# A reordered start and a tail taken by token block in an encoder block with product-key experts

## The chip, the cores and the metric

The kernel runs on one core of one Trainium2 chip. The metric is the device time of one execution in microseconds (us); lower is better. The core's engines run at the same time and are ordered by semaphores alone: PE (TensorE: matmuls, transposes), DVE (VectorE), ACT (ScalarE), POOL (GpSimd) and SP, which here only issues transfers. ACT and POOL issue transfers too.

## The reference

512 tokens of width 1024, float32. What it computes:

```python
h = layer_norm(x, ln_emb_g, ln_emb_b)
z = h @ w_in                          # 28 chunks of 128 columns
# gated short convolution: cb * conv3(cc * cx); 8 recurrent heads: two directions of
# conv4, two gates, h_t = a_t*h_{t-1} + sqrt(1-a_t^2)*i_t*x_t, with
# log a_t = -8 * r_t * softplus(-lambda)
mix = concat(rms_norm(gelu(gate) * lru), rms_norm(y_conv))
h = layer_norm(ALPHA * h + mix @ w_out, ln1_g, ln1_b)
# experts: per token and each of 8 query heads the best 16 of 128*128 experts by key sums
y = sum over the 128 chosen e of gate_e * gelu(h . u_e) * v_e
out = layer_norm(ALPHA * h + y, ln2_g, ln2_b)
```

## The kernel before, in words

Activations are split into four token blocks of 128. Products of float32 operands are made as three passes, hi*hi, hi*lo and lo*hi: ACT writes the rounded half of a tile ("hi"), another engine subtracts it to get the rest ("lo").

**Start and mixer** (`mixer`, lines 163 to 647). DVE takes moments of each token block (`stats`) and normalises it, POOL makes the inverse roots, PE turns the block (L135). ACT scales each of the eight 128x512 turned tiles (`shape`, L144), DVE splits each into hi (L150) and lo (L152). The first product `z_chunk(0)` takes each tile as it comes. The weights of chunk n come by SP into one of three buffers; ACT rounds them (`w_upper`, L339), and POOL subtracts (`w_lower`, L267). Chunks alternate between two PSUM banks, so chunk n waits until chunk n-2's bank has been read. Order of the chunks: four groups j of three (0 to 11) for the short convolution, then two for each head. In a group j, ACT copies the first chunk (L379), DVE multiplies it with the second (L477), convolves (L483, L485) and multiplies with the third (L487). Every engine works in program order. Ahead of group 0, DVE's program has the 21 small dependent operations for softplus of lambda (L456 to L467, 128x16 each), which only the heads use. POOL, beside `w_lower`, applies gain and shift to one token block in two operations (L295, L297) in chunks 2 to 9. The parameter vectors are turned by PE in one transpose each (L564, L565), put ahead of the last token block's transposes; ACT copies them out (L347, L348) after `w_upper(1)`, and the scaling needs them. The gain and shift rows of the first norm (`ln`) and the gate weights are issued on ACT's queue before its first rounding.

**Experts** (`experts`, from L1295). Token blocks 0 to 2 (`DT` = 3) are taken densely over all 128 blocks of 128 experts: 128 steps, each for one V block. A step makes w = activations * gates (DVE, L1571), rounds it (ACT, L1500) and the V block (ACT, L1481), subtracts (DVE, L1576 and L1549), and PE adds 18 matmuls of 128x512 (L1451) into six PSUM banks, two for each token block. V blocks have four slots (`SLOT`), so V block n+4 is rounded when step n's matmuls are done; v_hi and v_lo of n+2 are made in step n, ahead of the w halves of step n. Token block 3 goes by gathered rows: one gather in DVE's program at each step up to step 111; the next 16 steps have none.

**The end.** After the steps, DVE adds the gathered sums to block 3 (L1586, L1588), and then for each block in turn: two operations that add PSUM (L1596), moments (L1600, L1602); POOL makes scale and shift in four small operations (L1536 to L1539); ACT normalises (L1509); gain and shift are applied by DVE on 768 columns and by POOL on 256 (`affine`, L1378, L1379); SP stores. `y_ready` rises for a token block when its matmuls of the last step are done.

Of the kernel before, what the change touches and what calls it, by code (L numbers as in the profile page):

```python
# [22 lines left out]
F32 = mybir.dt.float32  # L23
# [8 lines left out]
P = 128  # L32
# [123 lines left out]
def mixer(nc, a, sem, bank, h, ident, ones, iota, small, pB):  # L156
    V, S, G = nc.vector, nc.scalar, nc.gpsimd
    with ExitStack() as st:
# [71 lines left out]
        with nc.Block() as block:  # L230
            @block.sync
            def _(eng):
                for tb in range(TB):
                    eng.dma_start(h[:, tb, :], a["x"][0, tb * P:(tb + 1) * P, :]).then_inc(x_loaded[tb], 16)
                for n, c in enumerate(order):
                    after(eng, w_lo_ready, n - NW + 1)
                    eng.dma_start(wbuf[n % NW][:, :, :],
                                  a["w_in"][0, :, c * P:(c + 1) * P].rearrange("(k p) c -> p k c", p=P)
                                  ).then_inc(w_loaded[n % NW], 16)
                    for c in rows_with(n):  # L240
                        eng.dma_start(wo[:, c, :], a["w_out"][0, c * P:(c + 1) * P, :]).then_inc(wo_loaded, 16)

            @block.gpsimd
            def _(eng):
# [68 lines left out]
            def _(eng):  # L313
# [13 lines left out]
                for i, name in enumerate(("ln_emb_g", "ln_emb_b")):  # L327
                    eng.dma_start(ln[:, i, :], a[name].partition_broadcast(P)).then_inc(ln_loaded, 16)
# [90 lines left out]
            def _(eng):  # L419
# [35 lines left out]
                eng.wait_ge(exp_lam, 2)  # L455
                link(V.tensor_scalar(out=s, in0=e, scalar1=2.0, scalar2=None, op0=ALU.add))  # L456
                link(V.reciprocal(s, s))
                link(V.tensor_tensor(out=s, in0=s, in1=e, op=ALU.mult))
                link(V.tensor_tensor(out=s2, in0=s, in1=s, op=ALU.mult))
                link(V.tensor_scalar(out=poly, in0=s2, scalar1=1.0 / 15, scalar2=1.0 / 13, op0=ALU.mult, op1=ALU.add))  # L460
                for k in (11, 9, 7, 5, 3, 1):
                    link(V.tensor_tensor(out=poly, in0=poly, in1=s2, op=ALU.mult))
                    link(V.tensor_scalar(out=poly, in0=poly, scalar1=1.0 / k, scalar2=None, op0=ALU.add))
                link(V.tensor_tensor(out=poly, in0=poly, in1=s, op=ALU.mult))
                link(V.tensor_scalar(out=neg, in0=neg, scalar1=0.0, scalar2=LRU_C / 2, op0=ALU.max, op1=ALU.mult))
                link(V.scalar_tensor_tensor(out=sp[:, 0, :], in0=poly, scalar=LRU_C, in1=neg, op0=ALU.mult, op1=ALU.add))
                V.tensor_scalar(out=sp[:, 1, :], in0=sp[:, 0, :], scalar1=-1.0, scalar2=None,  # L467
                                op0=ALU.mult).then_inc(sp_ready, 1)


                eng.wait_ge(xp_zero, 1)
                for j in range(CONV):
# [16 lines left out]
                    V.sem_inc(y_ready, 1)  # L489

# [801 lines left out]
def experts(nc, a, sem, bank, h, small, acts, far, act_dram, gates_dram, out):  # L1292
# [9 lines left out]
    STEPS = KEYS  # L1302
    GATHERS = 2 * TURN
# [4 lines left out]
    assert u_turns * GATHERS == SLOTS - U_FROM and 0 <= tail_tiles <= STEPS - TAIL  # L1308
    LAST = (DT, *range(DT))
    LEFT, RIGHT = slice(0, 6 * P), slice(6 * P, D)  # L1310
# [10 lines left out]
    with ExitStack() as st:  # L1321
# [13 lines left out]
        shift = sb("shift2", [P, TB, 1])  # L1335
# [7 lines left out]
        ln2_loaded, var_ready, rstd_ready, norm_ready, stored = (sem(n) for n in (  # L1343
            "ln2_loaded", "var2_ready", "rstd2_ready", "norm2_ready", "out_stored"))
        y_ready, left_ready, right_ready = sem("y_block_ready"), sem("out_left_ready"), sem("out_right_ready")
        chain, pool_chain = sem("dve_chain_experts"), sem("pool_chain_experts")
# [38 lines left out]
        with nc.Block() as block:  # L1385
            @block.sync
            def _(eng):
# [50 lines left out]
            def _(eng):  # L1438
                mm = nc.tensor.matmul

                def outputs(n, i):

                    first, last = (isinstance(n, int) and n == e for e in (0, STEPS - 1))
                    r = i % SLOT
                    eng.wait_ge(v_lo_ready, n + 1)
                    eng.wait_ge(w_lo_ready, n + 1)
                    for tb in range(DT):
                        for w, v, begins, ends in ((w_hi, v_hi, first, False), (w_hi, v_lo, False, False),
                                                   (w_lo, v_hi, False, last)):
                            for half in range(2):  # L1450
                                ins = mm(bank[2 + 2 * tb + half][:, :], w[r][:, tb * P:(tb + 1) * P],  # L1451
# [176 lines left out]
```

## Time and profile before

| | us |
|---|---|
| median of 3 runs | 1784.73 (1784.1 to 1785.97) |
| profiled execution, its own time | 1783.23 |
| its span, first to last instruction | 1781.4 |
| PE busy | 1683.2 (94%) |
| DVE busy | 1327.9 (75%) |
| ACT busy | 664.6 (37%) |
| POOL busy | 741.0 (42%) |
| mean granted TensorE clock | 0.973 of full speed |

Busy shares are means over stages with different limits. Where PE has no idle time, PE sets the pace, and nothing on another engine shortens the stage; where it is idle, the row tells what it waited for. Times on the rows below are us from the span's start.

### The profile page before, as it was taken

To read this page: it belongs to the slowest core of one execution; us is meant where nothing else is said; L and a number is where in the kernel's file an instruction comes from. 1 tells how busy PE (TensorE), PEld (TensorE's weight loads), DVE (VectorE), ACT (ScalarE), POOL (GpSimd) and SP (SyncE) were. 2 spreads that over 40 slices of the span, in tenths; PEclk is the share of its full clock that TensorE was granted. 3 is DMA by queue.
4 is the path that set the end of the run, shared out by engine and by line. 5 is a ranking of instruction groups with operands and counts; after the bars stand their busy time and mean duration, and the time that the engine had idled before them with its cause. 6 is when DMAs were issued, how large, how long until landed. Compare 5 with 4: busy or idle time off the path is not lost. (4 is left out here: it accounts for less than half of the span.)

```text
span 1781.4 us, 26976 instructions
## 1 busy us (share of the span) xinstructions
PE 1683.2 (94%) x8781; PEld 1462.4 (82%) x8781; DVE 1327.9 (75%) x2584; ACT 664.6 (37%) x1034; POOL 741.0 (42%) x690
## 2 busy tenths in 40 slices
PE   5999989799998999999999988999999999999995
PEld 4786644489998999899999987888888888888884
DVE  7469962458888888688779817778777778888756
ACT  3457760243334334233323323333333333333332
POOL 5635430194432211221145404444666667555303
PEclk8999999899999999999999998999999999999997
DMA  7422100333323666965988899999999989999971
GB/s 262 128 79 71 54 0 0 121 97 113 113 78 103 196 190 201 372 190 178 312 300 256 273 325 348 326 318 319 320 323 319 319 294 331 363 356 356 320 229 57
DMA packets 224427, 396.75 MB, mean 223 GB/s; under 512 B 15256, under 2 KB 155472, under 8 KB 224336
## 3 DMA queue, kind: packets, MB, share of 16 engines
q1 hardware_dynamic: 182512, 258.12, 43.2%
q0 software_dynamic: 36864, 134.23, 22.1%
q10 hardware_dynamic: 4960, 3.24, 0.6%
q8 instruction: 50, 0.82, 0.2%
q14 instruction: 41, 0.34, 0.1%
HBM read 349.40 MB, written 46.14 MB: 222 GB/s over the span
## 5 line engine op out<-in xcount | busy, mean ns | idle before, releaser
L709 PE MATMUL bank<-xhi,ut_hi 128*128 128x384 f32 x1024 | 355.6, 347 | 0.0
L709 PE MATMUL bank<-xhi,ut_lo 128*128 128x384 f32 x1024 | 344.4, 336 | 0.0
L709 PE MATMUL bank<-xlo,ut_hi 128*128 128x384 f32 x1024 | 344.4, 336 | 0.0
L801 POOL COPY row_index<-expert_rows 128x1 int32<-128x1 int32 (+1 forms) x256 | 158.3, 618 | 425.4 <-DVE gather_product L819 343.8
L1451 PE MATMUL bank<-v_hi,w_hi 128*128 128x512 f32 x768 | 241.0, 395 | 3.8 <-DVE w_lo L1576 3.8
L1451 PE MATMUL bank<-v_lo,w_hi 128*128 128x512 f32 x768 | 238.0, 391 | 0.0
L1451 PE MATMUL bank<-v_hi,w_lo 128*128 128x512 f32 x768 | 237.5, 391 | 0.0
L1481 ACT ACTIVATE v_hi<-v_raw 128x1024 fp32r<-128x1024 f32 x128 | 135.6, 1060 | 244.0 <-PE bank L1451 236.3
L767 DVE TENSOR_TENSOR ut_lo<-bank,ut_hi 128x512 fp32r<-128x512 f32 x216 | 141.5, 684 | 113.6 <-ACT ut_hi L726 112.4
L806 POOL DMA_INDIRECT gathered<-in_peer_v,row_index x128 | 179.4, 1401 | 106.2 <-POOLq L805 102.8
L1549 DVE TENSOR_TENSOR v_lo<-v_raw,v_hi 128x1024 fp32r<-128x1024 f32 x128 | 156.3, 1221 | 70.8 <-ACT v_hi L1481 70.8
L709 PEld LDWEIGHTS bank<-xlo,ut_hi 128*128 128x128 f32 x1024 | 194.1, 190 | 0.0
L709 PEld LDWEIGHTS bank<-xhi,ut_hi 128*128 128x128 f32 x1024 | 194.1, 190 | 0.0
L709 PEld LDWEIGHTS bank<-xhi,ut_lo 128*128 128x128 f32 x1024 | 193.4, 189 | 0.0
L806 POOL DMA_INDIRECT gathered<-in_peer_u,row_index x128 | 143.5, 1121 | 107.0 <-POOLq L805 101.9
L726 ACT ACTIVATE ut_hi<-bank 128x512 fp32r<-128x512 f32 x256 | 144.9, 602 | 78.2 <-PE bank L697 77.9
L697 PE MATMUL bank<-ident,u_raw 128*128 128x128 f32 x1024 | 142.6, 278 | 29.2 <-DVE ut_lo L767 14.7
L1451 PEld LDWEIGHTS bank<-v_lo,w_hi 128*128 128x128 f32 x768 | 144.8, 189 | 30.9
L1451 PEld LDWEIGHTS bank<-v_hi,w_lo 128*128 128x128 f32 x768 | 144.7, 188 | 30.9
L1451 PEld LDWEIGHTS bank<-v_hi,w_hi 128*128 128x128 f32 x768 | 142.6, 189 | 32.0 <-DVE v_lo L1549 4.2
L819 DVE SCALAR_TENSOR_TENSOR gather_product<-gathered,h 128x1024 f32<-128x1024 f32 x128 | 156.2, 1220 | 9.8 <-DMA gathered<-in_peer_u,row_index 4.7
L823 DVE SCALAR_TENSOR_TENSOR gather_sum<-gathered,expert_gates,gather_sum 128x1024 f32<-128x1024 f32 x128 | 160.5, 1278 | 2.5 <-DMA gathered<-in_peer_v,row_index 2.5
(182 smaller groups left out, 2697.7 us busy)
## 6 DMA issues: line engine op xcount, KB each, us to landing
u_raw<-in_peer_u SPq DMA_DIRECT2D x128, 512.0 KB, 4.8
v_raw<-in_peer_v SPq DMA_DIRECT2D x128, 512.0 KB, 6.0
g_in<-gate_matrix SPq DMA_DIRECT2D x128, 192.0 KB, 4.2
activations<-gel SPq DMA_DIRECT2D x96, 192.0 KB, 2.9
a_in<-activations SPq DMA_DIRECT2D x96, 192.0 KB, 4.5
gate_matrix<-stage SPq DMA_DIRECT2D x15, 1152.0 KB, 8.2
w_in<-in_w_in SPq DMA_DIRECT2D x28, 512.0 KB, 3.8
wq<-in_peer_wq SPq DMA_DIRECT2D x16, 512.0 KB, 4.2
```

The costliest lines, as they stand in the source:

```text
L697: ins = self.nc.tensor.transpose(self.bank[b][:, k * P:(k + 1) * P], raw[:, j * P:(j + 1) * P], self.ident[:, :])
L709: ins = self.nc.tensor.matmul(self.bank[b + (r % 2) * spare][:, 0:DTOK], u[r % 2][:, k, :], x[:, k, 0:DTOK], start=(i == 0), stop=(i == 3 ...
L726: ins = self.nc.scalar.activation(self.hi[r % 2][at], turned, ACT.Copy)
L767: self.nc.vector.tensor_tensor(out=self.lo[r % 2][at], in0=self.bank[b].rearrange("p (k e) -> p k e", k=4), in1=self.hi[r % 2][at].bitcast ...
L801: nc.gpsimd.tensor_copy(self.index[r][:, :], self.rows[:, bass.ds(k, 1)]).then_inc(self.index_ready, 1)
L806: nc.gpsimd.indirect_dma_start(out=self.tile[r][:, :], out_offset=None, in_=self.tables[kind], in_offset=bass.IndirectOffsetOnAxis(ap=self ...
L819: ins = V.scalar_tensor_tensor(out=self.product[:, :], in0=self.tile[r][:, :], scalar=1.0, in1=self.x, op0=ALU.mult, op1=ALU.mult, accum_o ...
L823: ins = V.scalar_tensor_tensor(out=y, in0=self.tile[r][:, :], scalar=self.gate[:, bass.ds(k, 1)], in1=y, op0=ALU.mult, op1=ALU.add)
L1451: ins = mm(bank[2 + 2 * tb + half][:, :], w[r][:, tb * P:(tb + 1) * P], v[r][:, half * HALF_D:(half + 1) * HALF_D], start=begins, stop=ends)
L1481: S.activation(v_hi[r][:, :], v_raw[r][:, :], ACT.Copy).then_inc(v_hi_ready, 1)
L1549: V.tensor_tensor(out=v_lo[r][:, :], in0=v_raw[r][:, :], in1=v_hi[r][:, :].bitcast(F32), op=ALU.subtract).then_inc(v_lo_ready, 1)
```

## The change

At the start: `w_lower(0)` and `w_lower(1)` go from POOL to DVE, the first ahead of the eight splits and the second between the fourth and the fifth. `w_upper(1)` goes behind the second scaled tile. The turns of the parameters go ahead of token block 2 in place of 3. The two `ln` transfers go to SP's queue behind the third weight transfer; the gate weights stay on ACT's queue, behind the eight scalings. The softplus goes from before group 0 to behind group 2.

At the end: the last four steps (`CLOSE` = 124) are multiplied by token block, all four V blocks for block 0, then 1, then 2, so that block 0's sums are final 48 matmuls before the last. For that, V block 127 is rounded and subtracted in step 126 behind w, not in 125. Token block 3 is finished in six parts in steps 112 to 117. The norm is on DVE, with POOL for the power alone: (h - mean) * gain in one operation, * root + shift in two halves, each stored as it comes; ACT has no part in it.

```diff
@@ -237,6 +237,9 @@
                     eng.dma_start(wbuf[n % NW][:, :, :],
                                   a["w_in"][0, :, c * P:(c + 1) * P].rearrange("(k p) c -> p k c", p=P)
                                   ).then_inc(w_loaded[n % NW], 16)
+                    if n == NW - 1:
+                        for i, name in enumerate(("ln_emb_g", "ln_emb_b")):
+                            eng.dma_start(ln[:, i, :], a[name].partition_broadcast(P)).then_inc(ln_loaded, 16)
...
@@ -282,11 +285,10 @@
                 for tb in range(TB):
                     invert_root(tb)
                 G.memset(xp[:, :, :], 0.0).then_inc(xp_zero, 1)
-                w_lower(0)
-                w_lower(1)
                 eng.wait_ge(ln_ready, 1)
                 eng.wait_ge(turner.turned, KD)
+                eng.wait_ge(w_lo_ready, 2)
...
-                for i, name in enumerate(("ln_emb_g", "ln_emb_b")):
-                    eng.dma_start(ln[:, i, :], a[name].partition_broadcast(P)).then_inc(ln_loaded, 16)
...
-                load_gate_weights(0)
-                load_gate_weights(1)
                 link = Chain(eng, act_chain)
                 w_upper(0)
-                w_upper(1)
                 eng.wait_ge(pT_ready, 1)
                 S.activation(pB[:, :], bank[7][:, last][:, 0:PC_END], ACT.Copy)
                 S.activation(pA[:, :], bank[6][:, last], ACT.Copy).then_inc(p_ready, 1)
                 eng.wait_ge(p_ready, 1)
                 for k in range(KD):
+                    if k == 2:
+                        w_upper(1)
                     turner.shape(eng, k)
+                load_gate_weights(0)
+                load_gate_weights(1)
...
+                def w_lower(n):
+                    eng.wait_ge(w_hi_ready, n + 1)
+                    V.tensor_tensor(out=w_lo[n % 2][:, :, :], in0=wbuf[n % NW][:, :, :],
+                                    in1=w_hi[n % 2][:, :, :].bitcast(F32), op=ALU.subtract).then_inc(w_lo_ready, 1)
+                w_lower(0)
                 for k in range(KD):
+                    if k == 4:
+                        w_lower(1)
                     turner.split(eng, k)
...
-                eng.wait_ge(exp_lam, 2)
-                link(V.tensor_scalar(out=s, in0=e, scalar1=2.0, scalar2=None, op0=ALU.add))
...
+                def softplus():
+                    eng.wait_ge(exp_lam, 2)
+                    link(V.tensor_scalar(out=s, in0=e, scalar1=2.0, scalar2=None, op0=ALU.add))
+                    link(V.reciprocal(s, s))
...
+                    if j == CONV - 2:
+                        softplus()
...
-                    if tb == TB - 1:
+                    if tb == TB - 2:
...
-                        if tb == TB - 1 and k == 6:
+                        if tb == TB - 2 and k == 6:
...
+    CLOSE = STEPS - SLOT
+    FAR_DONE = TAIL + tail_tiles
...
-        def affine(eng, engine, link, at, cols, ready):
-            blk = h[:, LAST[at], cols]
-            eng.wait_ge(norm_ready, at + 1)
-            link(engine.tensor_tensor(out=blk, in0=blk, in1=ln[:, 0, cols], op=ALU.mult))
-            engine.tensor_tensor(out=blk, in0=blk, in1=ln[:, 1, cols], op=ALU.add).then_inc(ready, 1)
...
-                    for cols, ready in ((RIGHT, right_ready), (LEFT, left_ready)):
-                        eng.wait_ge(ready, at + 1)
+                    for half in range(2):
+                        cols = slice(half * HALF_D, (half + 1) * HALF_D)
+                        eng.wait_ge(out_ready, 2 * at + half + 1)
                         eng.dma_start(out[0, tb * P:(tb + 1) * P, cols], h[:, tb, cols]).then_inc(stored, 16)
...
+                def block_outputs(tb, r, first, last):
+                    for w, v, begins, ends in ((w_hi, v_hi, first, False), (w_hi, v_lo, False, False),
+                                               (w_lo, v_hi, False, last)):
+                        for half in range(2):
+                            ins = mm(bank[2 + 2 * tb + half][:, :], w[r][:, tb * P:(tb + 1) * P],
+                                     v[r][:, half * HALF_D:(half + 1) * HALF_D], start=begins, stop=ends)
+                    return ins
+                def closing():
+                    for tb in range(DT):
+                        for n in range(CLOSE, STEPS):
+                            if tb == 0:
+                                eng.wait_ge(v_lo_ready, n + 1)
+                                eng.wait_ge(w_lo_ready, n + 1)
+                            ins = block_outputs(tb, n % SLOT, False, n == STEPS - 1)
+                        ins.then_inc(y_ready, 1)
...
-                outputs(STEPS - 1, STEPS - 1)
+                closing()
...
-                    if not (isinstance(n, int) and n + 2 >= STEPS):
+                    if not (isinstance(n, int) and n + 2 >= STEPS - 1):
...
+                    if isinstance(n, int) and n == STEPS - 2:
+                        v_upper(n + 1, i + 1, (n + 1) // SLOT + 1)
...
-                for at, tb in enumerate(LAST):
-                    eng.wait_ge(rstd_ready, at + 1)
-                    S.activation(h[:, tb, :], h[:, tb, :], ACT.Identity, scale=rs[:, tb, :],
-                                 bias=shift[:, tb, :]).then_inc(norm_ready, 1)
...
-                        link(G.tensor_tensor(out=rs[:, tb, :], in0=mv[:, tb, 1:2], in1=small[:, 2:3], op=ALU.add))
-                        link(G.tensor_tensor(out=rs[:, tb, :], in0=rs[:, tb, :], in1=small[:, 0:1], op=ALU.pow))
-                        link(G.tensor_tensor(out=shift[:, tb, :], in0=mv[:, tb, 0:1], in1=rs[:, tb, :], op=ALU.mult))
-                        G.tensor_tensor(out=shift[:, tb, :], in0=shift[:, tb, :], in1=small[:, 1:2],
-                                        op=ALU.mult).then_inc(rstd_ready, 1)
...
+                for at, tb in enumerate(LAST):
+                    eng.wait_ge(var_ready, at + 1)
+                    G.tensor_tensor(out=rs[:, tb, :], in0=rs[:, tb, :], in1=small[:, 0:1],
+                                    op=ALU.pow).then_inc(rstd_ready, 1)
...
-                    if not (isinstance(n, int) and n + 2 >= STEPS):
+                    if not (isinstance(n, int) and n + 2 >= STEPS - 1):
...
+                    if isinstance(n, int) and n == STEPS - 2:
+                        v_lower(n + 1, i + 1)
...
+                    if isinstance(n, int) and FAR_DONE <= n < FAR_DONE + 6:
+                        far_block(n - FAR_DONE)
+                link = Chain(eng, chain)
+                def moments(tb):
+                    for i in range(2):
+                        ins = V.bn_stats(bn[:, tb, i, :], h[:, tb, i * HALF_D:(i + 1) * HALF_D])
+                    link(ins)
+                    link(V.bn_aggr(mv[:, tb, :], bn[:, tb, :, :].rearrange("p a b -> p (a b)")))
+                    V.tensor_scalar(out=rs[:, tb, :], in0=mv[:, tb, 1:2], scalar1=LN_EPS, scalar2=None,
+                                    op0=ALU.add).then_inc(var_ready, 1)
+                def centre(tb):
+                    link(V.scalar_tensor_tensor(out=h[:, tb, :], in0=h[:, tb, :], scalar=mv[:, tb, 0:1], in1=ln[:, 0, :],
+                                                op0=ALU.subtract, op1=ALU.mult))
+                def spread(tb):
+                    eng.wait_ge(rstd_ready, LAST.index(tb) + 1)
+                    for half in range(2):
+                        cols = slice(half * HALF_D, (half + 1) * HALF_D)
+                        V.scalar_tensor_tensor(out=h[:, tb, cols], in0=h[:, tb, cols], scalar=rs[:, tb, :],
+                                               in1=ln[:, 1, cols], op0=ALU.mult, op1=ALU.add).then_inc(out_ready, 1)
+                def far_block(part):
+                    if part == 1:
+                        link(V.scalar_tensor_tensor(out=h[:, DT, :], in0=h[:, DT, :], scalar=ALPHA, in1=far.sum[0][:, :],
+                                                    op0=ALU.mult, op1=ALU.add))
+                    elif part == 2:
+                        link(V.tensor_tensor(out=h[:, DT, :], in0=h[:, DT, :], in1=far.sum[1][:, :], op=ALU.add))
+                    elif part == 3:
+                        moments(DT)
+                    elif part == 4:
+                        eng.wait_ge(ln2_loaded, 32)
+                        centre(DT)
+                    elif part == 5:
+                        spread(DT)
...
-                for at in range(TB + 1):
-                    if at < TB:
-                        tb = LAST[at]
-                        if at:
-                            eng.wait_ge(y_ready, at)
-                            for i in range(2):
-                                blk = h[:, tb, i * HALF_D:(i + 1) * HALF_D]
-                                ins = V.scalar_tensor_tensor(out=blk, in0=blk, scalar=ALPHA, in1=bank[2 + 2 * tb + i][:, :],
-                                                             op0=ALU.mult, op1=ALU.add)
-                            link(ins)
-                        for i in range(2):
-                            ins = V.bn_stats(bn[:, tb, i, :], h[:, tb, i * HALF_D:(i + 1) * HALF_D])
-                        link(ins)
-                        V.bn_aggr(mv[:, tb, :], bn[:, tb, :, :].rearrange("p a b -> p (a b)")).then_inc(var_ready, 1)
-                    if at:
-                        affine(eng, V, link, at - 1, LEFT, left_ready)
+                for tb in range(DT):
+                    eng.wait_ge(y_ready, tb + 1)
+                    for i in range(2):
+                        blk = h[:, tb, i * HALF_D:(i + 1) * HALF_D]
+                        ins = V.scalar_tensor_tensor(out=blk, in0=blk, scalar=ALPHA, in1=bank[2 + 2 * tb + i][:, :],
+                                                     op0=ALU.mult, op1=ALU.add)
+                    link(ins)
+                    moments(tb)
+                    centre(tb)
+                    spread(tb)
```

## Rows read from the trace of the kernel before

**Rows 1.** The page: an engine's busy time; a group, with mean ns.
```profile
PE 1683.2 (94%) x8781; PEld 1462.4 (82%) x8781; DVE 1327.9 (75%) x2584; ACT 664.6 (37%) x1034; POOL 741.0 (42%) x690
...
L1549 DVE TENSOR_TENSOR v_lo<-v_raw,v_hi 128x1024 fp32r<-128x1024 f32 x128 | 156.3, 1221 | 70.8 <-ACT v_hi L1481 70.8
```

**Rows 2.** Waits of PE, whole run: us in total, times, longest.
```profile
PE bank L585 <- DVEq L478: 7.9, 1, 7.9
```

**Rows 3.** Windows: length, busy time of each engine, PEclk, DMA share, GB/s.
```profile
39.50:47.50 8.00, 0.08 (x2) 0.04 (x1) 7.47 (x14) 1.06 (x1) 5.26 (x3) 0.63 0.91 314
47.50:51.50 4.00, 4.00 (x10) 3.13 (x11) 2.62 (x4) 0.00 (x0) 0.00 (x0) 0.50 0.38 146
```

**Rows 4.** Timeline, 29 to 47 us: start, length, engine, line, operation.
```profile
29.45 0.18 DVE L456 TENSOR_SCALAR t<-t 128x16 f32<-128x16 f32 x1 [0.28 <-ACT t L353]
...
30.54 2.40 POOL L267 TENSOR_TENSOR w_in_lo<-w_in,w_in_hi 128x1024 fp32r<-128x1024 f32 x1 [11.34 <-ACT w_in_hi L339]
...
30.57 2.39 DVE L462 TENSOR_TENSOR t<-t 128x16 f32<-128x16 f32 x1
...
46.48 0.17 DVE L467 TENSOR_SCALAR sp<-sp 128x16 f32<-128x16 f32 x1
```

**Rows 5.** Timeline of ACT, 34 to 56 us: roundings of weights.
```profile
34.17 1.06 ACT L339 ACTIVATE w_in_hi<-w_in 128x1024 fp32r<-128x1024 f32 x1 [3.32 <-PE bank L585]
39.61 1.06 ACT L339 ACTIVATE w_in_hi<-w_in 128x1024 fp32r<-128x1024 f32 x1 [4.38 <-PE bank L585]
55.23 1.06 ACT L339 ACTIVATE w_in_hi<-w_in 128x1024 fp32r<-128x1024 f32 x1 [14.56 <-PE bank L585]
```

**Rows 6.** Timeline of DVE around the end of group 2.
```profile
84.04 0.69 DVE L487 TENSOR_TENSOR y<-hd,bank 128x512 f32<-128x512 f32 x1
94.29 0.69 DVE L477 TENSOR_TENSOR xp<-dw,bank 128x512 f32<-128x512 f32 x1 [9.56 <-PE bank L585]
```

**Rows 7.** Timeline of POOL beside it.
```profile
83.56 2.72 POOL L267 TENSOR_TENSOR w_in_lo<-w_in,w_in_hi 128x1024 fp32r<-128x1024 f32 x1
89.91 2.41 POOL L267 TENSOR_TENSOR w_in_lo<-w_in,w_in_hi 128x1024 fp32r<-128x1024 f32 x1 [3.63 <-ACT w_in_hi L339]
```

**Rows 8.** Timeline, 12 to 28 us, of DVE.
```profile
13.26 1.42 DVE L431 TENSOR_SCALAR h<-h,mv,rs 128x1024 f32<-128x1024 f32 x1 [0.71 <-POOL rs L262]
17.90 1.58 DVE L150 CAST hT_hi<-dq 128x512 fp32r<-128x512 f32 x1 [3.21 <-ACT dq L144]
...
20.58 0.69 DVE L152 TENSOR_TENSOR hT_lo<-dq,hT_hi 128x512 fp32r<-128x512 f32 x1
...
26.95 0.69 DVE L152 TENSOR_TENSOR hT_lo<-dq,hT_hi 128x512 fp32r<-128x512 f32 x1
```

**Rows 9.** Timeline, 12 to 18 us, of PE, then of ACT.
```profile
14.74 0.87 PE L135 MATMUL bank<-ident,h 128*128 128x128 f32 x6
15.72 1.06 ACT L339 ACTIVATE w_in_hi<-w_in 128x1024 fp32r<-128x1024 f32 x1 [3.69 <-DMA w_in<-in_w_in]
```

**Rows 10.** Window over the last five steps.
```profile
1740.00:1759.70 19.70, 19.70 (x87) 15.97 (x86) 12.37 (x19) 4.65 (x7) 1.15 (x4) 1.00 0.06 18
```

**Rows 11.** Timeline of the halves of w in step 126.
```profile
1746.19 0.55 DVE L1571 TENSOR_TENSOR w<-a_in,g_in 128x384 f32<-128x384 f32 x1
...
1746.78 0.53 ACT L1500 ACTIVATE w_hi<-w 128x384 fp32r<-128x384 f32 x1 [1.81 <-DVE w L1571]
...
1747.34 0.56 DVE L1576 TENSOR_TENSOR w_lo<-w,w_hi 128x384 fp32r<-128x384 f32 x1 [0.59 <-ACT w_hi L1500]
```

**Rows 12.** Timeline of the end, 1753 to 1776 us.
```profile
1753.93 0.57 POOL L1537 TENSOR_TENSOR rs<-rs,small 128x1 f32<-128x1 f32 x1
...
1757.03 1.28 DVE L1596 SCALAR_TENSOR_TENSOR h<-h,bank 128x512 f32<-128x512 f32 x2 [3.56 <-PE bank L1451]
...
1760.83 1.28 POOL L1537 TENSOR_TENSOR rs<-rs,small 128x1 f32<-128x1 f32 x1
...
1774.74 1.32 POOL L1379 TENSOR_TENSOR h<-h,ln 128x256 f32<-128x256 f32 x1
```

More of the change, by code:

```diff
@@ L461, in _ @@
[L461 to L466, printed above, removed]
@@ L467, in _ @@
-                V.tensor_scalar(out=sp[:, 1, :], in0=sp[:, 0, :], scalar1=-1.0, scalar2=None,
-                                op0=ALU.mult).then_inc(sp_ready, 1)
+                def softplus():
+                    eng.wait_ge(exp_lam, 2)
+                    link(V.tensor_scalar(out=s, in0=e, scalar1=2.0, scalar2=None, op0=ALU.add))
+                    link(V.reciprocal(s, s))
+                    link(V.tensor_tensor(out=s, in0=s, in1=e, op=ALU.mult))
+                    link(V.tensor_tensor(out=s2, in0=s, in1=s, op=ALU.mult))
+                    link(V.tensor_scalar(out=poly, in0=s2, scalar1=1.0 / 15, scalar2=1.0 / 13, op0=ALU.mult, op1=ALU.add))
+                    for k in (11, 9, 7, 5, 3, 1):
+                        link(V.tensor_tensor(out=poly, in0=poly, in1=s2, op=ALU.mult))
+                        link(V.tensor_scalar(out=poly, in0=poly, scalar1=1.0 / k, scalar2=None, op0=ALU.add))
+                    link(V.tensor_tensor(out=poly, in0=poly, in1=s, op=ALU.mult))
+                    link(V.tensor_scalar(out=neg, in0=neg, scalar1=0.0, scalar2=LRU_C / 2, op0=ALU.max, op1=ALU.mult))
+                    link(V.scalar_tensor_tensor(out=sp[:, 0, :], in0=poly, scalar=LRU_C, in1=neg, op0=ALU.mult, op1=ALU.add))
+                    V.tensor_scalar(out=sp[:, 1, :], in0=sp[:, 0, :], scalar1=-1.0, scalar2=None,
+                                    op0=ALU.mult).then_inc(sp_ready, 1)
@@ L1307, in experts @@
     assert TURNS * SLOT == KEYS - MADE and GATHERS % RING == 0 and 2 < u_turns < TURNS - 1
-    assert u_turns * GATHERS == SLOTS - U_FROM and 0 <= tail_tiles <= STEPS - TAIL
+    FAR_DONE = TAIL + tail_tiles
+    assert u_turns * GATHERS == SLOTS - U_FROM and 0 <= tail_tiles and FAR_DONE + 6 <= CLOSE
     LAST = (DT, *range(DT))
-    LEFT, RIGHT = slice(0, 6 * P), slice(6 * P, D)
     is_live = lambda n, i: i % 2 == 0 and (not isinstance(n, int) or n < TAIL)
@@ L1334, in experts @@
         rs = sb("rs2", [P, TB, 1])
-        shift = sb("shift2", [P, TB, 1])
         v_loaded = [sem(f"v_loaded{i}") for i in range(SLOT)]
@@ L1342, in experts @@
         y_done = sem("y_step_done")
[L1343 to L1346, printed above, removed]
+        ln2_loaded, var_ready, rstd_ready, stored = (sem(n) for n in (
+            "ln2_loaded", "var2_ready", "rstd2_ready", "out_stored"))
+        y_ready, out_ready = sem("y_block_ready"), sem("out_half_ready")
+        chain = sem("dve_chain_experts")
         def steps(eng, step, between=lambda: None):
@@ L1441, in outputs @@
                 def outputs(n, i):
-                    first, last = (isinstance(n, int) and n == e for e in (0, STEPS - 1))
-                    r = i % SLOT
+                    first = isinstance(n, int) and n == 0
                     eng.wait_ge(v_lo_ready, n + 1)
@@ L1447, in outputs @@
                     for tb in range(DT):
[L1448 to L1451, printed above, removed]
-                                         v[r][:, half * HALF_D:(half + 1) * HALF_D], start=begins, stop=ends)
-                        if last:
-                            ins.then_inc(y_ready, 1)
-                    if not last:
-                        ins.then_inc(y_done, 1)
+                        ins = block_outputs(tb, i % SLOT, first, False)
+                    ins.then_inc(y_done, 1)
+                def block_outputs(tb, r, first, last):
[13 more added lines that the diff above has]
+                        ins.then_inc(y_ready, 1)
                 def step(n, i, t, tiles):
@@ L1466, in step @@
                             acts.turn_half(eng, 1, m + 1, r + 1, (r + 1) // acts.UB + 1 + t, 0, 0)
-                    if not (isinstance(n, int) and n == 0):
+                    if not (isinstance(n, int) and (n == 0 or n > CLOSE)):
                         outputs(n - 1, i - 1)
                 steps(eng, step)
-                outputs(STEPS - 1, STEPS - 1)
+                closing()
             @block.scalar
```

17 lines of the change are left out of this document (removed).

## The prediction

> **What bounds the kernel now.** I read the page's busy times first: PE is busy for 1683.2 of 1781.4 us [rows 1], so only what PE waits for, what it does slowly, and what lies behind its last matmul can be worth microseconds. The waits of PE come next. Among them one wait of 7.9 us at the head of a weight chunk stands for DVE's queue [rows 2]. The window around it shows PE with 0.08 us of work in 8.0 us while DVE is busy for 7.47, and in the 4.0 us behind it a granted clock of 0.50, that is 1.2 instead of 2.4 GHz [rows 3]. The timeline tells what DVE does there: the softplus, 21 dependent operations of 0.17 to 0.25 us that begin at 29.45 and end at 46.65 [rows 4]. Chunk 3 needs the bank that DVE's first product of group 0 reads, and this product stands behind the softplus. Last, the end: PE is done by 1759.7 [rows 10], the last result is there at 1776.06 [rows 12], the span ends at 1781.4.
>
> **The change part by part, the softplus.** Chunks 1 and 2 without a wait are 39.61 - 34.17 = 5.44 us apart by the roundings that follow them. Chunk 3 takes 55.23 - 39.61 = 15.62 us [rows 5]. With the softplus gone from its place, DVE has the product ready within a microsecond of chunk 1's end, some 4 us before chunk 3 wants the bank: 15.62 - 5.44 = **10.2 us** go, 8 of idle time and 2.2 of low clock. What is late next is `w_lower(3)` on POOL, and behind it in each chunk one of the gain or shift operations; a POOL operation of this size takes 2.4 to 2.7 us [rows 4, 7], so two of them fit a chunk of 5.44 by 0.0 to 0.6 us. I take nothing for it, as each is queued only behind the last, and keep 4 us (1 us in four chunks) as the bound below; 10.2 is the bound above.
>
> In its new place the softplus follows the last product of group 2, which ends at 84.04 + 0.69 = 84.73, and DVE is free until 94.29 [rows 6]. What it takes there: 21 steps of 0.21 are 4.4 us. It took 17.2 before, since POOL was at work nearly all that time: one small operation that begins 0.03 us behind a POOL operation of 2.40 us takes 2.39 us [rows 4]. Beside the new place POOL has two operations, 83.56 to 86.28 and 89.91 to 92.32 [rows 7], which can hold one small operation each: 4.4 + 1.6 + 2.4 = 8.4 us, under the 9.56 that are free. So nothing. Should it last longer, the product of group 3 can still be 5.4 us late, until chunk 12 wants its bank.
> The Trainium skill has this as a rule (SBUF — State Buffer, "Who interferes with whom"): DVE and GpSimd share a port pair that whoever starts first holds for the whole instruction, and the other fully blocks. The row of 2.39 beside 2.40 us agrees. By this rule the cost follows from the number of POOL operations in the window; if sharing slowed every small operation in proportion, the softplus would take its 17.2 us again and the sum would be the first rival's.
>
> **The start.** Now: normalisation of block 3 ends at 13.26 + 1.42 = 14.68; ACT rounds the second weights at 15.72, when they have landed, and scales only then, so that DVE's first split begins at 17.90 and takes 1.58 beside POOL; the later splits come every (26.95 - 20.58) / 6 = 1.06 us; the last ends at 27.64 [rows 8, 9]. After: `w_lower(0)` on DVE from 14.7; its nearest row is v_lo, the same shape and engine, 1.22 us [rows 1]: until 15.9. ACT has the parameters by then, because PE turned them two transposes earlier, and the first scaling can follow PE's turns from 14.74 on [rows 9]. Split 0 to 17.0, three more at 1.06 and about 0.3 for ACT's rounding of the second weights (1.06 us [rows 9]) between two scalings: 20.5. `w_lower(1)` to 21.7, four splits to 25.95. Gain 27.64 - 25.95 = **1.7 us**. The ends: the parameters' loads land only just before the time at which they are turned now (0.9 us later than I take), or chunk 0 runs wholly at the low clock (24 matmuls at 0.43 instead of 0.23 us, which ends 0.3 us behind the splits): 0.5. Without the 0.66 us by which block 3's normalisation is held, and with ACT's rounding hidden: 2.8. The edits that move work onto other queues cost nothing by this: SP's queue carries the `ln` rows (2 x 512 KB) ahead of the fourth weights, which it now issues only when `w_lo` 0 is done (15.9), and what uses `ln` comes after the splits. ACT issues four gate weight loads of 0.5 us behind the last scaling, 24.7 to 26.7, while its next work, the exponential, waits for DVE until about 27.4. If that cover were gone, each microsecond would come off the 1 us by which `w_lower(2)` is early for chunk 2. DVE's two subtractions are inside the sum above.
>
> **The end.** PE's 72 matmuls of the last four steps take 72 x 0.2265 us (87 in 19.70 us [rows 10]) = 16.3, so they begin at 1743.4. Block 0 wants V blocks 124, 125, 126 in 3 x 6 matmuls = 4.1 us and w and V of block 127 at 1747.5. Spacing w to w_hi to w_lo to the next w is 0.59, 0.56, 0.47 us [rows 11]. Step 125 no longer waits for V 127: w(125) at 1742.11, one step ahead of the 1746.19 of the row, then w_lo(125) 1743.26 (wanted 1744.8), w(126) 1743.73, w_hi 1744.32, V 127 rounded to 1745.9 (1.06), subtracted to 1747.1, w_lo(127) from 1748.2 to 1748.75. So PE waits **1.3 us** once; bounds 0 and 2.6 (each operation of this chain later by a semaphore). Then block 0 is final at 1750.2 and PE ends at 1761.0 instead of 1759.7.
> DVE from 1750.4: two additions of PSUM 1.32 (1.28 for the pair [rows 12]) and two moments, of the same size, 1.32; aggregate 0.24, epsilon 0.10, centre 1.23 (1024 columns, as v_lo [rows 1]), the root, two halves of output 0.60 each: the power takes 0.57 us alone, but 1.28 where DVE has operations on two SBUF tiles beside it [rows 12], so it is held until the centring ends and then takes some 0.5. Sum 5.9 us a block. That is more than PE's 24 matmuls (5.44), so DVE sets the end: 1750.4 + 3 x 5.9 = 1768.1. Before it was 1774.74 + 1.32 = 1776.06, for this stage is served serially, all four blocks and ACT and POOL in the chain. 8.0 us, and 0.4 for one transfer of 256 KB last in place of two of 128 and 384: **8.4 us**. Bounds: root hidden, so that PE sets the pace and only one block of 5.4 us follows 1761.0, 9.9; root wholly behind the centring (6.7 us a block) and the wait 2.6 us, 4.7. The six parts for block 3 lie in steps in which a gather of 1.2 to 1.3 us is missing from DVE; each part is at most 1.7 us, and the step has more idle time than the difference. If not, some tenths.
>
> **The sum** against the profiled execution: 1783.23 - 1.7 - 10.2 - 8.4 = 1762.9. The median of the runs shown is 1.5 above this execution: **1764.4 us**. All low ends give 0.5 + 6.2 + 4.7 = 11.4 (1773.3), all high ends 2.8 + 10.2 + 9.9 = 22.9 (1761.8).
>
> **Rivals.** First, the softplus doesn't fit its new place. For it: DVE's and POOL's operations interlock, and the wait of 17.2 us was made so. At 17.2 us it ends at 101.9, 2.2 us behind the 99.7 at which chunk 12 wants the bank; with the product 0.7 and a low clock of up to 2.2 us behind the gap, 3 to 5 us come back: 1767.4 to 1769.4, say 1768.4. Against it: only two POOL operations there. Second, the 11.9 us of the start are lost again later, as the stage of the heads or a stage with loads takes its pace from something that doesn't move. Then the end alone remains: 1784.7 - 8.4 = 1776.3. Against it: every load is issued after a semaphore of the work before it, so all of it moves together. Third, slower: the clock. PE got 1.2 GHz after the gap [rows 3], and with chunk 0 now paced by splits that pause for `w_lower(1)`, it might stay there. Each chunk of 24 matmuls costs 24 x 0.2 = 4.8 us more; the change is slower once this lasts over four chunks, and at six it stands at 1764.4 + 28.8 = 1793.2. Against it: chunk 3 is back at full speed before its end.
>
> **How the numbers follow.** Forecast 0.77 (its own range 1760 to 1768), first rival 0.12, second 0.07, third 0.04. The range for 8 in 10 takes forecast and first rival and the ends of the unknown costs: from the high ends' 1761.8, less the 1.9 us over which the three runs spread, to the low ends' 1773.3, so 1760 to 1773. About 0.2% (3.6 us) is what a measurement of this kernel can tell from no change. Faster by more: forecast and the first two rivals, 0.95; within it: 0.01, a mix of second rival and a dear end; slower: 0.04.
>
> **What would show it.** Chunk 3's matmuls follow chunk 2's without a gap and at 2.4 GHz; the softplus lies between two group products and takes 7 to 9 us; the last split ends near 26; one wait of about 1.3 us in the first token block of the closing; three DVE rounds of 5.9 us, the power beginning with the centring and ending behind it. The prediction is wrong if PE shows a new wait over 2 us in chunks 1 to 12, or if the DVE rounds take over 6.5 us.

## The result and the profile after

The changed kernel takes 1764.49 us in the median of 4 runs (1762.95 to 1766.34); before 1784.99 (1784.1 to 1785.97, 4 runs). The ratio is 0.9882, with a 95% interval from 0.9871 to 0.9894: 20.5 us or 1.2% less. A second set of runs gave 1765.04 and 0.9873 (0.9858 to 0.9888).

The profiled execution took 1766.34 us itself, the slowest of its four, with a span of 1764.5; that of before, at 1783.23, was faster than all four timed ones. So the two spans stand only 16.9 us apart. The part of the traces that makes this difference is told at the end of this section.

The page of after, beside [rows 1]:

```profile
PE 1676.8 (95%) x8781; PEld 1456.0 (83%) x8781; DVE 1329.9 (75%) x2594; ACT 659.4 (37%) x1030; POOL 730.2 (41%) x668
```

**The softplus.** ACT's roundings of weights in the trace of after; the three shown follow chunks 2, 3 and 12:

```profile
37.51 1.06 ACT L339 ACTIVATE w_in_hi<-w_in 128x1024 fp32r<-128x1024 f32 x1 [4.38 <-PE bank L598]
42.95 1.06 ACT L339 ACTIVATE w_in_hi<-w_in 128x1024 fp32r<-128x1024 f32 x1 [4.38 <-PE bank L598]
...
93.71 1.06 ACT L339 ACTIVATE w_in_hi<-w_in 128x1024 fp32r<-128x1024 f32 x1 [4.24 <-PE bank L598]
```

Before, the roundings that follow chunks 0 and 12:

```profile
29.32 1.05 ACT L339 ACTIVATE w_in_hi<-w_in 128x1024 fp32r<-128x1024 f32 x1
...
105.99 1.06 ACT L339 ACTIVATE w_in_hi<-w_in 128x1024 fp32r<-128x1024 f32 x1 [4.24 <-PE bank L585]
```

The step of 15.62 of [rows 5] is now 5.44, like its neighbours. The rounding at 93.71 stood at 105.99 before: the program gets through the first chunk of the heads 12.3 us earlier. Of these, 2.1 are there at chunk 0 already (27.22 against 29.32), and 10.2 come between the two marks. The window [rows 3] has no mate any more: from 28 to 110 us PE waits for nothing. DVE in the new place of the softplus, beside [rows 6] (start, length, line), with one operation of POOL:

```profile
65.92 2.41 POOL L270 TENSOR_TENSOR w_in_lo<-w_in,w_in_hi 128x1024 fp32r<-128x1024 f32 x1 [0.73 <-ACT w_in_hi L339]
...
66.05 2.56 DVE L494 TENSOR_SCALAR hd<-xp,pB 128x512 f32<-128x512 f32 x1 [0.57 <-DVE xp L488]
...
74.28 0.69 DVE L498 TENSOR_TENSOR y<-hd,bank 128x512 f32<-128x512 f32 x1
75.23 0.17 DVE L468 TENSOR_SCALAR t<-t 128x16 f32<-128x16 f32 x1 [0.26 <-DVE y L498]
...
77.82 2.27 DVE L475 TENSOR_SCALAR t<-t 128x16 f32<-128x16 f32 x1
...
81.59 0.17 DVE L479 TENSOR_SCALAR sp<-sp 128x16 f32<-128x16 f32 x1
82.01 0.69 DVE L488 TENSOR_TENSOR xp<-dw,bank 128x512 f32<-128x512 f32 x1 [0.24 <-PE bank L598]
```

The 21 operations take from 75.23 to 81.76, 6.5 instead of 17.2 us, and one of them is held, for 2.27 us. Group 2's last product ended late, 10.2 us after its first (64.79 to 74.97) instead of 7.7, as one more of its operations met POOL (2.56 us at 66.05). The same two operations before, where the group's first product began at 77.07:

```profile
77.91 0.49 DVE L483 TENSOR_SCALAR hd<-xp,pB 128x512 f32<-128x512 f32 x1 [0.16 <-DVE xp L477]
...
78.19 2.46 POOL L267 TENSOR_TENSOR w_in_lo<-w_in,w_in_hi 128x1024 fp32r<-128x1024 f32 x1 [0.74 <-ACT w_in_hi L339]
```

POOL's operation stands where it stood, 1.1 us behind the group's first product. DVE's begins 0.4 us later than before, now just behind POOL's instead of just ahead of it, and is held. This is so in all six traces with the whole new start and in none of the other five; what delays it is not shown. So the softplus ended only 0.25 us before group 3's product could begin.

**The start.** DVE and then ACT, beside [rows 8, 9]:

```profile
12.93 1.42 DVE L432 TENSOR_SCALAR h<-h,mv,rs 128x1024 f32<-128x1024 f32 x1 [0.71 <-POOL rs L265]
14.27 1.20 DVE L444 TENSOR_TENSOR w_in_lo<-w_in,w_in_hi 128x1024 fp32r<-128x1024 f32 x1
15.66 0.43 DVE L150 CAST hT_hi<-dq 128x512 fp32r<-128x512 f32 x1 [0.19 <-ACT dq L144]
...
24.86 0.69 DVE L152 TENSOR_TENSOR hT_lo<-dq,hT_hi 128x512 fp32r<-128x512 f32 x1
```

```profile
14.85 1.45 ACT L144 ACTIVATE dq<-bank,pB 128x512 f32<-128x512 f32 x2 [1.81 <-PE bank L135]
```

The scalings begin at 14.85, the weights are subtracted on DVE in 1.20 us, the first split begins at 15.66 and the last ends at 25.55; before, 27.64. Block 3's normalisation begins at 12.93 instead of 13.26; in the eleven traces it begins at 12.93 to 13.26, so this third of a microsecond is not the edit's. From it to the rounding behind chunk 0 it is 14.3 us instead of 16.1: 1.8 us are the edit's. A window over chunk 0, of after and then of before (the last three numbers are PEclk, DMA share, GB/s):

```profile
20.00:24.00 4.00, 2.58 (x9) 1.45 (x9) 3.90 (x8) 2.04 (x3) 0.00 (x0) 1.00 0.64 216
```

```profile
20.30:24.30 4.00, 3.95 (x9) 3.14 (x10) 3.86 (x8) 3.11 (x4) 0.00 (x0) 0.50 1.06 362
```

Chunk 0 ran at 2.4 GHz; before, its first 4 us were at 1.2. Ahead of its first matmul PE had been idle for 1.45 us, before for 2.8. From 17 to 21 us, the granted clock is 1.00 in all seven traces with the reordered start and 0.50 to 0.73 in the four with the old one.

**The end.** PE's only wait in the closing, POOL's power, and DVE's rounds, beside [rows 12]:

```profile
1740.68 0.69 PE L1462 MATMUL bank<-v_hi,w_hi 128*128 128x512 f32 x2 [1.34 <-DVE w_lo L1583]
```

```profile
1745.47 1.52 POOL L1548 TENSOR_TENSOR rs<-rs,small 128x1 f32<-128x1 f32 x1 [45.57 <-DVE rs L1600]
```

```profile
1739.98 0.56 DVE L1583 TENSOR_TENSOR w_lo<-w,w_hi 128x384 fp32r<-128x384 f32 x1 [0.59 <-ACT w_hi L1518]
1742.34 1.28 DVE L1638 SCALAR_TENSOR_TENSOR h<-h,bank 128x512 f32<-128x512 f32 x2 [1.81 <-PE bank L1462]
...
1745.30 1.28 DVE L1605 SCALAR_TENSOR_TENSOR h<-h,mv,ln 128x1024 f32<-128x1024 f32 x1
1747.10 1.42 DVE L1613 SCALAR_TENSOR_TENSOR h<-h,rs,ln 128x512 f32<-128x512 f32 x2 [0.52 <-POOL rs L1548]
1748.43 1.28 DVE L1638 SCALAR_TENSOR_TENSOR h<-h,bank 128x512 f32<-128x512 f32 x2
...
1759.25 1.42 DVE L1613 SCALAR_TENSOR_TENSOR h<-h,rs,ln 128x512 f32<-128x512 f32 x2 [0.52 <-POOL rs L1548]
```

The last half of w is ready at 1740.54, PE waits 1.34 us, and DVE's rounds begin at 1742.34, 1748.43 and 1754.50, 6.08 us apart. The last result is there at 1760.67, and the span ends 3.8 us later, instead of 5.3.

**Where the two traces differ besides.** The rounding of the first V block, by the tile's rows (count, durations, first and last start), of after and of before:

```profile
L1499 ACT ACTIVATE v_hi<-v_raw x128: 1046/1061/1065, 1057.6 to 1736.6; 128x1024 fp32r<-128x1024 f32 x128
```

```profile
L1481 ACT ACTIVATE v_hi<-v_raw x128: 1047/1061/1065, 1067.3 to 1743.5; 128x1024 fp32r<-128x1024 f32 x128
```

Here the lead is 9.7 us, after 12.3 at the heads. In step 124, it is 8.1 (V block 126 is rounded at 1731.28 against 1739.41), and the new end adds 8.8. The traces of the experiments tell whether the 4.2 us in between are the change's.

### The profile page after: what moved, and what is told of

Same layout as the page of the kernel before. It is cut to its first block and busy times, and to the rows that moved or that the text cites. A ratio compares the mean times of both kernels' runs of the same rounds, so it can differ in the third digit from the quotient of the medians.

```text
span 1764.5 us, 26964 instructions
## 1 busy us (share of the span) xinstructions
PE 1676.8 (95%) x8781; PEld 1456.0 (83%) x8781; DVE 1329.9 (75%) x2594; ACT 659.4 (37%) x1030; POOL 730.2 (41%) x668
## 5 line engine op out<-in xcount | busy, mean ns | idle before, releaser
L710 PE MATMUL bank<-ident,u_raw 128*128 128x128 f32 x1024 | 141.3, 276 | 30.9 <-DVE ut_lo L780 12.3
```

The source lines that it names most:

```text
L710: ins = self.nc.tensor.transpose(self.bank[b][:, k * P:(k + 1) * P], raw[:, j * P:(j + 1) * P], self.ident[:, :])
```

## The experiments

**The start alone, the end alone.**

```diff
 start_only: mixer() of after, experts() of before
 end_only:   mixer() of before, experts() of after
```

> The kernel before with the whole reordered start and the old end. Theory A (the parts add up, nothing behind the start gives time back): the two traces put the roundings that follow chunk 13 at 105.99 and 93.71 us, so 12.3 us less than before, about 1772.7. Theory B (the stages behind the start give back part of it: the same two traces stand 12.3 us apart at the heads and only 8.1 us apart at the last four steps): 8 us less, about 1777. In the trace, the gap of 7.9 us ahead of chunk 3 is gone under both.

Measured: 1774.95 us (6 runs, 1770.35 to 1777.61) against 1785.84 of before (17 runs); ratio 0.9939 (0.9926 to 0.9951), 10.9 us less. (The rounding that the expectation puts behind chunk 13 is the one behind chunk 12.)

> The kernel before with the new end alone. Theory A: the end is worth what the trace of the changed kernel shows behind the last four steps' begin, 8.8 us, about 1776.2, and the end is the same to 0.1 us: one wait of 1.3 us on PE, three rounds of 6.1 us on DVE. Theory B about the start says the same here; a rival for the end (part of its gain comes from the phase in which the shifted program meets its loads) gives 5 to 7 us.

Measured: 1776.88 us; ratio 0.9950 (0.9937 to 0.9963), 9.0 us less. The product of the two ratios is 0.9889, and the whole gave 0.9882 and 0.9873: the parts add up. Theory B's 8 us for the start are below the interval (8.8 to 13.2), and the next row shows what misled it. The first V block's rounding in the trace of the end alone, whose program is that of before up to there:

```profile
L1486 ACT ACTIVATE v_hi<-v_raw x128: 1045/1061/1065, 1070.7 to 1747.4; 128x1024 fp32r<-128x1024 f32 x128
```

The same program reaches this point at 1067.3 in one execution and at 1070.7 in another. Of the six traces with the whole new start it is reached at 1055.5 to 1060.8, mean 1058.2; the two old ones have a mean of 1069.0. The lead is 10.8 on the mean, where it was 12.7 at chunk 12 on the mean of the same traces. From chunk 12's rounding to this one, before took 961.3 us, the shortest of all eleven traces; the ten others took 961.8 to 966.9, with the softplus in its old place (963.9, 964.5 and 963.9) as well as in its new one. So the loss in the pair above is within what the stage varies by, and the traces cannot tell 1.9 us of loss from none. The same holds for the 1.6 us behind it: from this rounding to that of V block 126, before took 672.1 and after 673.7, and the eleven traces 670.7 to 673.7.

**The softplus alone, the reordered start alone.**

```diff
 softplus_only: before, and
+                def softplus():            # the 21 operations, unchanged
...
+                    if j == CONV - 2:
+                        softplus()
 reorder_only: mixer() of after, and
-                    if j == CONV - 2:
-                        softplus()
+                softplus()                 # ahead of group 0
```

> The kernel before with the 21 small operations moved behind group 2 and nothing else. Theory A: 15.62 - 5.44 = 10.2 us less, about 1774.8, chunk 3 right behind chunk 2 at 2.4 GHz. Rival (the wait ahead of chunk 3 would be taken over by POOL's subtraction, and the early start is what gives POOL its slack): 6 to 8 us less.

Measured: 1773.9 us; ratio 0.9933 (0.9921 to 0.9946), 11.9 us less. Its roundings behind chunks 2 and 3 (5.44 apart) and chunk 12:

```profile
39.37 1.06 ACT L339 ACTIVATE w_in_hi<-w_in 128x1024 fp32r<-128x1024 f32 x1 [4.38 <-PE bank L587]
44.81 1.06 ACT L339 ACTIVATE w_in_hi<-w_in 128x1024 fp32r<-128x1024 f32 x1 [4.38 <-PE bank L587]
...
95.57 1.06 ACT L339 ACTIVATE w_in_hi<-w_in 128x1024 fp32r<-128x1024 f32 x1 [4.24 <-PE bank L587]
```

105.99 - 95.57 = 10.4 us by the trace, of which 0.2 were there at chunk 0 (29.10 against 29.32), so 10.2 between the two marks. The rival's 6 to 8 us are below the interval (9.6 to 14.1). The softplus in this trace, its two held operations and group 3's product behind it:

```profile
74.57 1.32 DVE L457 TENSOR_SCALAR t<-t 128x16 f32<-128x16 f32 x1 [0.26 <-DVE y L487]
...
79.57 2.36 DVE L466 TENSOR_SCALAR t<-t 128x16 f32<-128x16 f32 x1
...
83.87 0.69 DVE L477 TENSOR_TENSOR xp<-dw,bank 128x512 f32<-128x512 f32 x1 [1.52 <-PE bank L587]
```

With only this edit made, POOL's operations at 73.15 and 79.49 hold one each, the softplus takes 7.8 us (74.57 to 82.34), and 1.5 are to spare.

> The kernel before with all of the reordered start but the softplus, which stays ahead of group 0. Theory A: all of the start moves by 2.1 us and the wait of about 8 us ahead of chunk 3 stays: 2.1 us less, about 1782.9. Rival (the softplus meets POOL's operations at another phase and ends at the same time as before): 0 to 1 us less.

Measured: 1784.73 us in 11 runs; ratio 0.9996 (0.9988 to 1.0005), 0.7 us less, from 2.1 less to 0.9 more. The wait stays; PE's waits of this run, and its transposes of the parameters:

```profile
PE bank L597 <- DVEq L490: 7.9, 1, 7.9
```

```profile
12.72 0.48 PE L576 MATMUL bank<-ident,prow 128*128 128x128 f32 x1 [0.59 <-DMA prow<-in_lru_lambda]
...
13.41 3.50 PE L135 MATMUL bank<-ident,h 128*128 128x128 f32 x16
```

This trace gained only 1.25 us (the rounding after chunk 0 at 28.07 against 29.32; in the six other traces with the new start 27.22 to 27.39). PE waited 0.59 us for the last of the twelve parameter loads, and its transposes end 1.4 us later (16.91 against 15.51). The late load alone doesn't explain it. PE waits 0.4 to 0.5 us for it in three of the six other traces too, and they lose nothing. Start_only:

```profile
12.69 0.33 PE L577 MATMUL bank<-ident,prow 128*128 128x128 f32 x1 [0.53 <-DMA prow<-in_lru_lambda]
...
13.15 1.09 PE L135 MATMUL bank<-ident,h 128*128 128x128 f32 x8
```

Its turns behind the wait take 1.09 us for eight, against 3.50 for sixteen in reorder_only, and its rounding after chunk 0 stands at 27.24. In after the turns are slow as well (2.96 for sixteen), but it has no wait. So the loss is there only where the late load and slow turns come together; why the turns are slow in some executions, at a granted clock of 1.00 in all three, is not shown. Beside 11.9 for the softplus and 10.9 for both, the timed runs cannot tell the reordering's share from zero; the traces show it up to the heads.

**POOL's other work taken away.**

```diff
 pool_quiet: before, and
-                    if n // 2 <= TB:       # L295, L297: gain and shift
...
+                    if n // 2 <= TB and n % 2 == 1:
+                        eng.sem_inc(h_ready, 1)
```

> The kernel before, with the softplus in its old place, and without POOL's gain and shift on the residual in chunks 2 to 9 (this part of the computation is left out; its time is read for the softplus alone). If each POOL operation holds at most one of DVE's small operations for its whole length, the softplus now meets one or two of the weight subtractions (2.4 us each) in place of seven operations: it takes 4.4 us and 2.4 to 4.8, so 7 to 9 us instead of 17.2, ends by 38.5 and PE's wait ahead of chunk 3 is gone. Rival (the small operations are slow for themselves, one after another at 0.8 us): 17 us, and the wait stays 7.9.

Measured: one run, 1774.38 us, the span 1772.6. DVE's softplus in its old place (first operation, the two held ones, the last), and then POOL:

```profile
29.18 0.17 DVE L452 TENSOR_SCALAR t<-t 128x16 f32<-128x16 f32 x1 [0.28 <-ACT t L349]
...
30.31 2.38 DVE L458 TENSOR_TENSOR t<-t 128x16 f32<-128x16 f32 x1
...
35.23 2.25 DVE L461 TENSOR_SCALAR t<-t 128x16 f32<-128x16 f32 x1
...
37.73 0.17 DVE L463 TENSOR_SCALAR sp<-sp 128x16 f32<-128x16 f32 x1
```

```profile
30.27 2.39 POOL L267 TENSOR_TENSOR w_in_lo<-w_in,w_in_hi 128x1024 fp32r<-128x1024 f32 x1 [11.34 <-ACT w_in_hi L335]
35.03 2.42 POOL L267 TENSOR_TENSOR w_in_lo<-w_in,w_in_hi 128x1024 fp32r<-128x1024 f32 x1 [2.38 <-ACT w_in_hi L335]
```

8.7 us instead of 17.2. The two operations that are held, 2.38 and 2.25 us, are those beside the two POOL operations, which begin at 30.27 and 35.03; all others take 0.17 to 0.25. PE's wait ahead of chunk 3 is gone. The softplus was slow by POOL alone, one operation held for each of POOL's. The count in before fits too, though the expectation has it one too high: beside the softplus stand six POOL operations (30.54 to 45.38), and six of the 21 are held, for 2.25 to 2.39 us each. Fifteen at 0.21 and six at 2.34 make the 17.2.

**The order of the closing, DVE's order in it, the root.**

```diff
 no_closing: after, and
-                closing()
+                for tb in range(DT):      # the last step; outputs(n - 1) in every step before it
+                    block_outputs(tb, (STEPS - 1) % SLOT, False, True).then_inc(y_ready, 1)
 w_first: after, DVE's step 127
+                    if isinstance(n, int) and n == STEPS - 1:
+                        v_lower(n, i)     # behind w of 127, not at the end of step 126
 root_first: after, centre()
+                    eng.wait_ge(rstd_ready, LAST.index(tb) + 1)
```

> The changed kernel itself once more, as the mate of the others of this job. Theory A: the same 20.5 us less than before (about 1764.5), and the lead over the trace of before at the first rounding of V blocks somewhere between 9.7 and 12.3 us, since the loss there (2.6 us in the first trace) is the spread of loads between executions. Theory B: again 9.7 us there.

Measured: 1765.04 us, ratio 0.9873 (0.9858 to 0.9888), 22 us less. The lead at the first V rounding was 8.7 us in this trace: below what theory A expected. It was set against the one trace of before that is early there; against the mean of both it is 10.4.

> The changed kernel with the last four steps in the old order, V block by V block; the norm on DVE and the early finish of token block 3 stay. DVE's first round can begin only when block 0's matmuls of step 127 are done, 13.7 us behind the begin of step 124, instead of 7.2: 6.5 us slower than the changed kernel, 1771.0, so that of the end's 8.8 us the order gives 6.5 and the shorter norm 2.3. Rival (the gain of the end is mostly the norm's): 2 to 3 us slower.

Measured: 1773.33 us, ratio to before 0.9924 (0.9910 to 0.9938): 8.3 us slower than the repetition. By the traces, with V block 126's rounding as the common point (1727.72 here, 1731.28 in after), DVE's first round begins 17.6 us later than it, not 11.1:

```profile
1745.34 1.29 DVE L1641 SCALAR_TENSOR_TENSOR h<-h,bank 128x512 f32<-128x512 f32 x2 [8.36 <-PE bank L1462]
```

6.6 us, as expected; the timed difference of 8.3 has some 3 us of uncertainty. From V block 126's rounding to the end of the span it is 39.8 us here, 42.0 before and 33.2 in after, so the norm's part of the end's 8.8 is 2.2.

> The changed kernel with DVE's order changed for the last V block: w of block 127 is made before V block 127 is subtracted, so that ACT rounds w while DVE subtracts V. If PE's wait of 1.34 us in the closing is the chain V subtract, w, round, subtract: the last half of w is ready at about 1739.4 instead of 1740.5 us of the changed kernel's trace, the wait shrinks to about 0.2 us, and, as DVE's rounds follow from block 0, the whole gets 1.1 us faster than the changed kernel, 1763.4. Rival (the wait is V block 127's load or PE's order): no change.

Measured: 1765.79 us, ratio 0.9884 (0.9868 to 0.9899); against the repetition's 0.9873 no gain can be told. The trace has it: PE's wait in the closing is

```profile
1739.92 0.70 PE L1462 MATMUL bank<-v_hi,w_hi 128*128 128x512 f32 x2 [0.19 <-DVE w_lo L1585]
```

0.19 us, the first round begins 9.9 us behind V block 126's rounding (1731.67) instead of 11.1, and the last result comes 28.3 us behind it instead of 29.4. So the wait was the chain that the prediction named, and 1.1 us is less than what two executions differ by.

> The changed kernel, where DVE waits for the root before it centres, so that POOL's power runs with DVE at rest. If the centring with its two SBUF tiles is what holds the power (1.52 us each time): the power takes 0.57 us, the outputs follow the centring at once, and a round takes 6.3 instead of 6.08 us, 0.7 us more in all. Rival (the power is slow for itself, or its operand is slow to come): it stays near 1.5 us and a round takes 7.2 us, 3.5 us more.

Measured: one run, 1768.23 us. POOL's power and DVE's first two rounds:

```profile
1747.80 0.56 POOL L1548 TENSOR_TENSOR rs<-rs,small 128x1 f32<-128x1 f32 x1 [45.55 <-DVE rs L1600]
```

```profile
1744.68 1.28 DVE L1639 SCALAR_TENSOR_TENSOR h<-h,bank 128x512 f32<-128x512 f32 x2 [1.79 <-PE bank L1462]
...
1748.39 1.28 DVE L1606 SCALAR_TENSOR_TENSOR h<-h,mv,ln 128x1024 f32<-128x1024 f32 x1 [0.68 <-POOL rs L1548]
...
1751.04 1.28 DVE L1639 SCALAR_TENSOR_TENSOR h<-h,bank 128x512 f32<-128x512 f32 x2
```

The power takes 0.56 instead of 1.52 us, and a round 6.36 instead of 6.08; from V block 126's rounding to the last result it is 30.2 us instead of 29.4, the 0.7 expected. One run can't show 0.7 us in the whole time. The centring is what holds it. The order of the changed kernel is the better one all the same, as it hides most of the root.

## Why the prediction was right

It said 1764.4 us and 20.3 less; measured were 1764.5 and 20.5. The mechanism held in each part; that the time is met to 0.1 us is luck, as the interval of the gain reaches from 18.9 to 23.0 us and the program varies by several us between executions. Step by step:

- **The softplus, 10.2 us.** 10.2 between the marks of chunks 0 and 12 in the trace of the edit alone, 11.9 (9.6 to 14.1) in its runs. What carried the step was the difference of two distances between roundings in one trace, which has the idle time and the low clock in one number. The prediction calls the 21 operations 0.17 to 0.25 us long; in before that holds for 15 of them.
- **Its new place.** Expected 8.4 us in 9.56 free ones, 1.2 to spare. With the softplus alone moved, it was 7.8 and 1.5. In the changed kernel it took 6.5, as it met only one POOL operation, but only because group 2 ended 2.5 us later in relation to its begin, and 0.25 was to spare. One operation held for each of POOL's is what all four traces show (pool_quiet above all); that another operation of DVE's would begin 0.4 us late and be held too had no term, and that the rest still fitted was luck. Had it come out 2 us worse, the 5.4 us of slack behind it would have taken it. The first rival falls by this.
- **The start, 1.7 us.** 2.1 in the trace of after, 1.8 of it counted from the normalisation of block 3; 1.25 in the trace of reorder_only. The parameters' loads, which the prediction named for its low end, were late in four of the seven traces and cost something in one only. The timed runs do not resolve this step.
- **PE's wait in the closing, 1.3 us.** 1.34. w_first shows that it is the chain V subtract, w, round, subtract.
- **DVE's round, 5.9 us.** 6.08: the power was held through all of the centring and ended 0.4 us behind it, as taken; most of the rest is the two output halves, 1.33 to the next operation where 1.2 was taken. DVE, not PE, sets the end.
- **The end, 8.4 us.** 8.8 in the trace, 9.0 (6.6 to 11.3) in the runs of the end alone. The results come 7.3 us earlier, where 8.0 was taken (three rounds longer by 0.2), and what lies behind them is 1.5 us shorter, where 0.4 was taken: two errors that cancel.
- **The second rival** (the start's gain is lost again) falls by start_only's 10.9 us. Whether a smaller part is lost, up to some 3 us by that interval, stays open. **The third** (the clock) went the other way: chunk 0 kept 2.4 GHz.

## What to carry to other kernels

In these traces, a chain of small dependent operations on DVE costs one of POOL's long operations for each of these that it meets (six, two, two and one); count those beside the chain's own length, put the chain where few of them stand, and leave some slack behind it, for half a microsecond of shift adds or removes one. If the last products can be ordered by the block that is finished, the tail begins earlier by the matmuls that the later blocks still have, and the next bound is the engine that does the tail: here 6.08 us a block against PE's 5.44. The value of an edit is best read as a distance between two marks close to it in one trace, since the same program varied by several us between executions.

## What was not expected of the hardware

The out projection begins at either clock. The 28 matmuls of the stage before the first mean squares, and the windows over it, of after and of its repetition, the same program:

```profile
240.37 12.28 PE L655 MATMUL bank<-wo,y 128*128 128x512 f32 x28 [2.22 <-ACT th L414]
230.00:254.00 24.00, 21.78 (x62) 10.19 (x61) 8.18 (x11) 10.72 (x15) 7.15 (x6) 1.00 0.00 1
```

```profile
240.44 13.98 PE L655 MATMUL bank<-wo,y 128*128 128x512 f32 x28 [2.21 <-ACT th L414]
230.00:254.00 24.00, 21.79 (x47) 9.29 (x46) 8.26 (x11) 10.80 (x15) 7.15 (x6) 0.91 0.00 0
```

The granted clock is 1.00 in one and 0.91 in the other, where it is 0.50 (1.2 GHz) from 242 to 244 us. The same matmuls take 12.28 and 13.98 us. DVE's wait for PE ahead of the first use of the mean squares is 8.22 us in after and 9.91 in the repetition. So 1.7 us more stand beside a lower clock, right behind a place where PE had been waiting 2.2 us for ACT in both, and with nothing changed in the program. Over the eleven traces, this wait of DVE's has two lengths only: 8.22 us in seven, before among them, and 9.88 to 9.91 in four. No run here holds the clock fixed, so that the clock alone makes the difference is the reading of these rows, and what decides between the two levels is not shown.
